# Attention units of two heads from each of two kv halves, in a two-layer decoder trunk on one core

## The reference, cut to what matters

```python
# SEQ 512, 16 query heads of 64, 4 kv heads, blocks of 128 queries, each sees 256 keys
s = einsum('bnqgrd,bnkgd->bngrqk', qb, kb) * HEAD_DIM ** -0.5
s = where(mask, s, NEG_INF)
m = maximum(max(s, axis=-1), sink)          # sink: one learned number per head
p = exp(s - m)
p = p / (sum(p, axis=-1) + exp(sink - m))
o = einsum('bngrqk,bnkgd->bnqgrd', p, vb)
```

## Time and profile before

| | us |
|---|---|
| median of three runs (3655.76 to 3673.56) | 3664.95 |
| span of the profiled execution, first to last instruction | 3662.8 |
| TensorE busy in it | 3550.3 (97%) |
| VectorE busy | 3128.9 (85%) |
| ScalarE busy | 1581.8 (43%) |
| the 16 units of the first layer, about 163 to 334 | 170.6 |
| the 16 units of the second layer, about 1979 to 2149 | 169.8 |

### The profile page before, as it was taken

The page is one execution under the profiler, slowest core; times in us unless marked ns, Lnnn a source line. Parts: engine busy times, 40 slices in busy tenths (PEclk is TensorE's granted clock), DMA queues, the critical chain, the costliest instruction groups (busy, mean ns, idle before and its releaser), DMA issues.

```text
span 3662.8 us, 61258 instructions
## 1 busy us (share of the span) xinstructions
PE 3550.3 (97%) x19206; PEld 3257.2 (89%) x19206; DVE 3128.9 (85%) x6312; ACT 1581.8 (43%) x2335; POOL 1393.5 (38%) x1140
## 2 busy tenths in 40 slices
PE   6999999999999999999999999999999999999999
PEld 5766788999999989999977667789999999999999
DVE  6899877999899878888868997779998987888888
ACT  4474434444455433333345644334444454333333
POOL 0000003575565534454500000036765655444543
PEclk9999999999999999999999999999999999999999
DMA  5111263467999899999921112635689999999998
GB/s 194 60 52 58 81 252 111 140 196 256 338 349 331 297 321 340 353 342 349 332 86 58 52 64 95 244 104 159 192 295 342 333 328 301 355 349 343 349 345 284
DMA packets 408601, 863.49 MB, mean 236 GB/s; under 512 B 165520, under 2 KB 231056, under 8 KB 407952
## 3 DMA queue, kind: packets, MB, share of 16 engines
q1 hardware_dynamic: 297456, 539.62, 44.2%
q0 software_dynamic: 73728, 268.47, 20.9%
q10 hardware_dynamic: 37152, 52.45, 3.9%
HBM read 774.41 MB, written 85.98 MB: 235 GB/s over the span
## 4 chain that ended last, share of the span: by engine, by line
issue 50%; PE 28%; POOL 17%; DMA 2%; DVE 2%; POOLq 0%; SPq 0%; ACT 0%; DVEq 0%; ACTq 0%
PE ps L829 8%; PE ps L830 8%; PE ps L831 8%; POOL w_lo L512 7%; POOL gbuf L528 5%; POOL spare L542 4%; PE ps L579 2%; PE ps L580 2%; PE ps L578 2%; DMA raw<-stream 1%; PE ps L803 1%; DMA cg<-gelu_scratch 1%; DMA gbuf<-u_rows,ids_u 0%; DVE oneR L1730 0%; DVE w_lo L1767 0%
## 5 line engine op out<-in xcount | busy, mean ns | idle before, releaser
L893 ACT CAST w_hi<-raw 128x1024 fp32r<-128x1024 f32 x680 | 715.8, 1055 | 871.0 <-DMA raw<-stream 821.5
L578 PE MATMUL ps<-h_hi,w_hi 128*128 128x384 f32 (+1 forms) x2944 | 1063.8, 361 | 3.5 <-DVE qT L1459 1.4
L580 PE MATMUL ps<-h_hi,w_lo 128*128 128x384 f32 (+1 forms) x2944 | 1037.7, 352 | 0.0
L579 PE MATMUL ps<-h_lo,w_hi 128*128 128x384 f32 (+1 forms) x2944 | 1036.4, 352 | 0.0
L829 PE MATMUL ps<-cf_hi,w_hi 128*128 128x384 f32 x2048 | 692.5, 338 | 13.2 <-DVE w_lo L1767 6.9
L830 PE MATMUL ps<-cf_lo,w_hi 128*128 128x384 f32 x2048 | 690.6, 337 | 0.0
L831 PE MATMUL ps<-cf_hi,w_lo 128*128 128x384 f32 x2048 | 690.5, 337 | 0.0
L542 POOL TENSOR_TENSOR spare<-spare 128x1 f32<-128x1 f32 x504 | 347.7, 690 | 851.6 <-DVE y_sp L1746 491.0
L578 PEld LDWEIGHTS ps<-h_hi,w_hi 128*128 128x128 f32 x2944 | 555.0, 189 | 58.2 <-issue 16.2
L579 PEld LDWEIGHTS ps<-h_lo,w_hi 128*128 128x128 f32 x2944 | 555.0, 189 | 38.9 <-issue 5.7
L580 PEld LDWEIGHTS ps<-h_hi,w_lo 128*128 128x128 f32 x2944 | 554.1, 188 | 37.5
(11 more groups left out here) (247 smaller groups left out, 4923.8 us busy)
## 6 DMA issues: line engine op xcount, KB each, us to landing
raw<-stream SPq DMA_DIRECT2D x682, 512.0 KB
gelu_scratch<-g_out ACTq DMA_DIRECT2D x256, 192.0 KB
cg<-gelu_scratch SPq DMA_DIRECT2D x256, 192.0 KB
c_scratch<-stage SPq DMA_DIRECT2D x64, 512.0 KB
cg<-c_scratch SPq DMA_DIRECT2D x256, 128.0 KB
qT<-ada SPq DMA_DIRECT2D x32, 512.0 KB
cgate<-ada SPq DMA_DIRECT2D x32, 512.0 KB
w_rows<-ada SPq DMA_DIRECT2D x32, 512.0 KB
```

What stands on the lines that cost most here:

```text
L578: nc.tensor.matmul(ps[:, b, 0:n], wh, hi[:, c, t0:T], start=c == 0, stop=False)
L579: nc.tensor.matmul(ps[:, b, 0:n], wh, lo[:, c, t0:T], start=False, stop=False)
L580: mm = nc.tensor.matmul(ps[:, b, 0:n], wl, hi[:, c, t0:T], start=False, stop=c == C - 1)
L893: nc.scalar.copy(w_hi[:, s], raw[:, s]).then_inc(hi_done, 1)
```

## The change

A unit is now one block `n`, one group `p`, and two query heads (`pair`) of each of its two kv heads. It still holds four heads. Three things follow.

- `scores` issues its four matmuls on alternating halves of the array's rows: partitions 0 to 63, 64 to 127, 0 to 63, 64 to 127. The two halves write to different banks.
- `values` multiplies two heads of each kv head: twice as many matmuls of half the columns (256 instead of 512), alternating between output partitions 0 to 63 and 64 to 127. The copies out of bank 6 (`attended_high` on ScalarE, `attended_low` on VectorE) are 128 partitions by 256 instead of 64 by 512.
- In `masked` the four scale-and-mask instructions and the reduction of the row maximum become four instructions that scale, mask and accumulate the maximum, each with a read of the accumulator, behind one small memset.

```diff
-    return n, 2 * p + half, p, half, half * HEAD
+    return n, p, pair
...
-                    for r in range(R):
-                        mm = nc.tensor.matmul(ps[:, 2 + r // 2, (r % 2) * 256 + own(n):(r % 2) * 256 + 256],
-                                              qT[lo64:lo64 + HEAD, p * R + r, n * P:(n + 1) * P],
-                                              kT[lo64:lo64 + HEAD, p, n * P + own(n):(n + 2) * P],
+                    for q in range(2):
+                        for half in range(2):
+                            rows64 = slice(half * HEAD, (half + 1) * HEAD)
+                            mm = nc.tensor.matmul(ps[:, 2 + half, q * 256 + own(n):q * 256 + 256],
+                                                  qT[rows64, p * R + 2 * pair + q, n * P:(n + 1) * P],
+                                                  kT[rows64, p, n * P + own(n):(n + 2) * P],
...
-                        mm = nc.tensor.matmul(ps[lo64:lo64 + HEAD, 6], vn[:, n + kb, g * HEAD:(g + 1) * HEAD],
-                                              pT[:, kb].rearrange("k r q -> k (r q)"),
+                        for half in range(2):
+                            head = (2 * p + half) * HEAD
+                            mm = nc.tensor.matmul(ps[half * HEAD:(half + 1) * HEAD, 6, 0:2 * P], vn[:, n + kb, head:head + HEAD],
+                                                  pT[:, kb, 2 * half:2 * half + 2].rearrange("k r q -> k (r q)"),
...
-                    nc.scalar.copy(o_hi[lo64:lo64 + HEAD, p * R:(p + 1) * R, n * P:(n + 1) * P],
-                                   ps[lo64:lo64 + HEAD, 6].rearrange("f (r q) -> f r q", r=R)).then_inc(o_hid, 1)
+                    nc.scalar.copy(o_hi[:, c:c + 2, n * P:(n + 1) * P],
+                                   ps[:, 6, 0:2 * P].rearrange("f (r q) -> f r q", r=2)).then_inc(o_hid, 1)
...
-                    for r in range(R):
-                        col = 2 * R * n + 2 * r + half
-                        ins = nc.vector.scalar_tensor_tensor(
-                            out=sc[:, r], in0=ps[:, 2 + r // 2, (r % 2) * 256 + own(n):(r % 2) * 256 + 256],
-                            scalar=rq[:, p, col:col + 1], in1=mask, op0=ALU.mult, op1=ALU.add)
+                    nc.vector.memset(spare[:, 0:1], 0.0)
+                    for s in range(R):
+                        half, q = s // 2, s % 2
+                        col = 2 * R * n + 2 * (2 * pair + q) + half
+                        ins = nc.vector.tensor_tensor_reduce(
+                            out=sc[:, s], in0=ps[:, 2 + half, q * 256 + own(n):q * 256 + 256], in1=mask,
+                            scale=rq[:, p, col:col + 1], scalar=LOWEST, op0=ALU.add, op1=ALU.max,
+                            accum_out=sm[:, 0, s:s + 1])
                     ins.then_inc(s_msk, 1)
                     dve.wait_ge(s_msk, k)
-                    nc.vector.tensor_reduce(sm[:, 0], sc, AX, ALU.max).then_inc(a_max, 1)
-                    dve.wait_ge(a_max, 2 * (l * UNITS + u) + 1)
-                    nc.vector.tensor_tensor(sm[:, 5], sm[:, 0], sink, ALU.max).then_inc(a_max, 1)
+                    nc.vector.tensor_tensor(two(sm[:, 5]), two(sm[:, 0]), sink, ALU.max).then_inc(a_max, 1)
...
-                    nc.vector.tensor_tensor(o_lo[dst], ps[lo64:lo64 + HEAD, 6].rearrange("f (r q) -> f r q", r=R),
+                    nc.vector.tensor_tensor(o_lo[dst], ps[:, 6, 0:2 * P].rearrange("f (r q) -> f r q", r=2),
                                             o_hi[dst].bitcast(F32), ALU.subtract).then_inc(o_lod, 1)
```

More of the change, by code:

```diff
@@ L112, in unit @@
 def unit(u):
-    p, n, half = u // (2 * NB), u // 2 % NB, u % 2
-    return n, 2 * p + half, p, half, half * HEAD
+    p, n, pair = u // (2 * NB), u // 2 % NB, u % 2
+    return n, p, pair
 def own(n):
@@ L641, in scores @@
                 def scores(u):
-                    n, g, p, half, lo64 = unit(u)
+                    n, p, pair = unit(u)
                     if u == 0:
@@ L649, in scores @@
                         pe.wait_ge(s_msk, l * UNITS + u)
-                    for r in range(R):
-                        mm = nc.tensor.matmul(ps[:, 2 + r // 2, (r % 2) * 256 + own(n):(r % 2) * 256 + 256],
-                                              qT[lo64:lo64 + HEAD, p * R + r, n * P:(n + 1) * P],
-                                              kT[lo64:lo64 + HEAD, p, n * P + own(n):(n + 2) * P],
-                                              start=True, stop=True)
+                    for q in range(2):
[4 more added lines that the diff above has]
+                                                  kT[rows64, p, n * P + own(n):(n + 2) * P],
+                                                  start=True, stop=True)
                     mm.then_inc(s_mm, 1)
@@ L679, in values @@
                         pe.wait_ge(p_ev, l * 2 * UNITS + 2 * u + kb + 1)
-                        mm = nc.tensor.matmul(ps[lo64:lo64 + HEAD, 6], vn[:, n + kb, g * HEAD:(g + 1) * HEAD],
-                                              pT[:, kb].rearrange("k r q -> k (r q)"),
-                                              start=kb == int(n == 0), stop=kb == 1)
+                        for half in range(2):
+                            head = (2 * p + half) * HEAD
+                            mm = nc.tensor.matmul(ps[half * HEAD:(half + 1) * HEAD, 6, 0:2 * P], vn[:, n + kb, head:head + HEAD],
+                                                  pT[:, kb, 2 * half:2 * half + 2].rearrange("k r q -> k (r q)"),
+                                                  start=kb == int(n == 0), stop=kb == 1)
                     mm.then_inc(o_mm, 1)
@@ L959, in attended_high @@
                 def attended_high(u):
-                    n, g, p, half, lo64 = unit(u)
+                    n, p, pair = unit(u)
+                    c = p * R + 2 * pair
                     act.wait_ge(o_mm, l * UNITS + u + 1)
-                    nc.scalar.copy(o_hi[lo64:lo64 + HEAD, p * R:(p + 1) * R, n * P:(n + 1) * P],
-                                   ps[lo64:lo64 + HEAD, 6].rearrange("f (r q) -> f r q", r=R)).then_inc(o_hid, 1)
+                    nc.scalar.copy(o_hi[:, c:c + 2, n * P:(n + 1) * P],
+                                   ps[:, 6, 0:2 * P].rearrange("f (r q) -> f r q", r=2)).then_inc(o_hid, 1)
                 for i in range(I_Q + C):
@@ L1379, in masked @@
                 def masked(u):
-                    n, g, p, half, lo64 = unit(u)
+                    n, p, pair = unit(u)
                     sc, sm = scores_sb[u % 2][:, :, own(n):], st[:, u % 2]
                     mask = con[:, K_MASK + own(n):K_MASK + 256]
-                    sink = lp[:, O_SK + g * R:O_SK + (g + 1) * R]
+                    two = lambda x: x.rearrange("q (h r) -> q h r", h=2)
+                    sink = two(lp[:, O_SK + 2 * p * R:O_SK + 2 * (p + 1) * R])[:, :, 2 * pair:2 * pair + 2]
                     k = l * UNITS + u + 1
@@ L1391, in masked @@
                         dve.wait_ge(p_tr, l * 2 * UNITS + 2 * u - 2)
-                    for r in range(R):
-                        col = 2 * R * n + 2 * r + half
-                        ins = nc.vector.scalar_tensor_tensor(
-                            out=sc[:, r], in0=ps[:, 2 + r // 2, (r % 2) * 256 + own(n):(r % 2) * 256 + 256],
-                            scalar=rq[:, p, col:col + 1], in1=mask, op0=ALU.mult, op1=ALU.add)
+                    nc.vector.memset(spare[:, 0:1], 0.0)
[6 more added lines that the diff above has]
+                            accum_out=sm[:, 0, s:s + 1])
                     ins.then_inc(s_msk, 1)
                     dve.wait_ge(s_msk, k)
-                    nc.vector.tensor_reduce(sm[:, 0], sc, AX, ALU.max).then_inc(a_max, 1)
-                    dve.wait_ge(a_max, 2 * (l * UNITS + u) + 1)
-                    nc.vector.tensor_tensor(sm[:, 5], sm[:, 0], sink, ALU.max).then_inc(a_max, 1)
-                    dve.wait_ge(a_max, 2 * (l * UNITS + u) + 2)
-                    nc.vector.tensor_tensor(sm[:, 3], sink, sm[:, 5], ALU.subtract).then_inc(a_den, 1)
+                    nc.vector.tensor_tensor(two(sm[:, 5]), two(sm[:, 0]), sink, ALU.max).then_inc(a_max, 1)
+                    dve.wait_ge(a_max, l * UNITS + u + 1)
+                    nc.vector.tensor_tensor(two(sm[:, 3]), sink, two(sm[:, 5]), ALU.subtract).then_inc(a_den, 1)
                     nc.vector.tensor_scalar(sm[:, 1], sm[:, 5], -1.0, None, ALU.mult).then_inc(a_neg, 1)
@@ L1413, in attended_low @@
                 def attended_low(u):
-                    n, g, p, half, lo64 = unit(u)
+                    n, p, pair = unit(u)
+                    c = p * R + 2 * pair
                     dve.wait_ge(o_hid, l * UNITS + u + 1)
-                    dst = (slice(lo64, lo64 + HEAD), slice(p * R, (p + 1) * R), slice(n * P, (n + 1) * P))
-                    nc.vector.tensor_tensor(o_lo[dst], ps[lo64:lo64 + HEAD, 6].rearrange("f (r q) -> f r q", r=R),
+                    dst = (slice(0, P), slice(c, c + 2), slice(n * P, (n + 1) * P))
```

(1 more changed line is left out.)

## The result

The changed kernel takes 3612.48 us (median of four runs, 3604.49 to 3618.99) against 3660.36 us (four runs) before: a ratio of 0.9864, 95% interval 0.9838 to 0.9890, so 1.36% faster, 48 us by the medians and 50 by the ratio.

The account below looks back on a forecast made before the run. TensorE was taken to bound the first half of each layer's attention units, VectorE the second. Savings of 9 and 8 us a layer, 34 for two, less 2 for the clock, gave 3633 us by the median, range 3618 to 3656.

Parts of the forecast that it names:

- What bounds the stage: Attention units: TensorE bounds the first half at 10.48 us a unit, VectorE the second at about 11.2 us.
- VectorE's part: Masked steps and low output parts: 1.38 us saved a full unit, 0.84 a light one, 19.9 us a layer.
- TensorE's part: Scores and values: overlapping array halves cut a full unit from 10.48 to about 9.1 us.
- my five slots: Eight records of scores, likewise values: alternating halves need five start slots instead of eight, saving 0.69 us in a full unit.
- The four slots that I worked out by the Trainium skill: Scores and values: the bound with all pairs running at once, saving 0.92 us; the forecast took five slots.
- The sum: Both halves of the units: 17 us a layer, 34 for two, less 2 for the clock; 3633 us by median.
- I take 9: First half of a layer's units, TensorE's: 9 us saved, from 9.7 for scores and values.
- I take 8: Second half of a layer's units, VectorE's: 8 us saved, from 8.8 for masked steps and low parts.
- took off 2 more for the clock: Both layers: 2 us less gain for a clock that falls where TensorE waits a little in more places.
- Without overlap: Rival in the units: array halves don't overlap, TensorE's 10.48 us bounds every unit; 3647 us, chance 0.2.
- A dear combined instruction: Rival in the masked step: combined instruction takes 0.66 instead of 0.39 us, no gain there; 3659 us, chance 0.1.
- Switches that empty the array: Rival in scores and values: each change of half costs 0.15 to 0.34 us, up to 3707 us; chance 0.07.

Follow-up runs that it names:

- the two runs with a TensorE unit of 10.49 us: Kernel before with the combined scale, mask and maximum instruction alone: 3640.56 us; changed kernel with four unread matmuls added in every unit: 3645.05 us.

## Why the forecast was right in its parts and wrong in its sum

**What bounds the stage: right.** TensorE first, VectorE in the second part, waits on the masked step. Undoing either engine's part alone leaves what the other allows (3648 and 3641).

**VectorE's part: right, the size a little low.** Forecast 19.9 us of work a layer. VectorE is busy 42.6 us less in the whole span, 21.3 a layer: the low part gives 0.27 (175.44 is the next start), a full masked step 1.20 instead of 1.11, a light one 0.68 instead of 0.57. From the first low part of the output to the last it took 332.83 - 176.40 = 156.4 us before and now

```profile
175.11 0.42 DVE L1425 TENSOR_TENSOR o_lo<-ps,o_hi 128x256 fp32r<-128x256 f32 x1
...
310.36 0.42 DVE L1425 TENSOR_TENSOR o_lo<-ps,o_hi 128x256 fp32r<-128x256 f32 x1 [0.58 <-ACT o_hi L967]
```

135.25 us: 21.2 less. Of these, 18.8 are work (busy 150.6 before, 131.7 now; three of the masked steps lie ahead of this stretch) and 2.3 are shorter pauses.

**TensorE's part: the mechanism right, the size low.** Four slots instead of five, 1.7 us a unit instead of 1.38. The order of the records, on which my five slots rested, has no say. The four slots that I worked out by the Trainium skill (TensorE: Matmul & The Clock Gate, Packing small matmuls) are what this trace shows: 1.13 and 1.08 us.

**The sum: this is the step that failed.** I split the stage at its middle, wrote "I take 9" for a TensorE half and "I take 8" for a VectorE half, and took off 2 more for the clock: 32 us for both layers. Measured from step to step, the halves gave 12.5 and 10.5 us in layer one, 13.3 and 10.1 in layer two. The first half is fuller by the four slots (12 x 0.86 and 4 x 0.43 are 12.0 us, an estimate from the full unit's saving), but that is not why the total was short: with 0.43 us added to each of TensorE's units, as by my five slots, the first half gave only 8.7 us, the second gave 15.0, and the sum stayed. A first half that ends later leaves VectorE less late, and TensorE meets that lateness in the second half. So the halves are not two sums with a limit each. As long as TensorE's unit is the shorter one, all that VectorE saves counts over the whole stage, in the first half too, where it was busy 78.6 of 82.8 us.

That alone would have made it 3665 - 2 x 19.9 = 3625, still 13 us above what was measured. VectorE's work fell by 2.8 us more than forecast in both layers together. The other terms, in the places where they came out in layer one: 21.2 between the low parts, where I had 17 for all of the stage. Ahead of the first low part 176.40 - 175.11 = 1.3 us were saved, where `scores(2)` runs at the lower clock (3.26 us before, 2.08 now). Behind the last one the next projection tile ends 1.9 us closer (341.1 - 332.8 before, 316.8 - 310.4 now), since TensorE idles 1.10 us there instead of 1.96 and the clock keeps its upper level. That is 24.4 us in layer one. In layer two the same three are 21.4, 1.7 and 0.4, together 23.5. The two give 47.8 of the 53.5 us by which the profiled spans differ (the medians differ by 47.9). The other 5.7 lie in layer one behind its units, where nothing was changed. From the last low part of layer one to the first transposes of layer two it is 1645.0 us in the profile of before, 1637.4 in that of the changed kernel, 1635.5 to 1642.9 in the nine other runs that leave the low parts there alone, and 1643.3 to 1646.5 in the three that move them. From the last low part of layer two to the end of the span it is 1514.3 and 1514.0 us in these two, and 1510.9 to 1523.7 over all runs. So I take it for variation from run to run, which is argued and not shown.

**The clock.** I took off 2 us for it. In layer one the granted clock stands at 0.50 twice behind the start of the units, from 243.9 to 247.3, right behind the 1.87 us wait above, and from 301.9 to 305.3; the second part has 0.96 against 0.98 before. In a stage that VectorE paces this costs next to nothing: in the run with one added matmul the clock is 1.00 from 169.6 to the end of the units, and the stage is only 0.7 us shorter (134.5 against 135.25), though TensorE has more to do in it.

**The rivals.** Without overlap: priced at 3647, measured as 3641 and 3645 in the two runs with a TensorE unit of 10.49 us. A dear combined instruction: 0.41 us against the 0.66 that rival needed. Switches that empty the array: there is no such price, neighbours start together.

## What to carry to other kernels

When two engines are nearly full and one may run several microseconds late before the other notices, don't take limits stretch by stretch: add up each engine's work over the whole run of steps, and the longer sum, with some pauses, is the time (here 3 to 6 us on 129 to 151). A shortening of one engine counts down to the sum of the other, so price both ends of a change together. Before work goes to an idle engine, look at what its instructions read: in this kernel an idle GpSimd was no free engine for VectorE's work, since most VectorE instructions beside it read two inputs from SBUF.

## What the runs showed of the hardware

- Matmuls on 64 rows of the array at partition 0 and at partition 64, and those with 64 output partitions at 0 and at 64, run fully side by side in float32: eight records of 256 columns in 1.13 and 1.08 us. Before it was 1.99 for the same eight records of `scores` on one half, and 1.93 for the same products of `values` as four records of 512. The order in which the halves are issued made no difference over four records.
- An instruction that scales from memory, adds and accumulates a maximum over 256 columns from PSUM starts every 0.41 us, and its accumulator read is hidden behind the next one's start.
- While GpSimd ran a 2.37 us subtraction with two SBUF inputs, a VectorE instruction of 4 columns with two SBUF inputs lasted 1.84 us instead of 0.16; two taps with two SBUF inputs each lasted 3.53 us instead of 1.41, and those with one PSUM and one SBUF input lasted 0.48 as always.
